# Attention stage of a hybrid decoder layer: which value products run whole in f32 (two key tiles in five, or every second one)

## What is computed

```python
s = einsum('bgrqd,bgnd->bgrqn', qi, ck) * scale
p_c = masked_softmax(s, cmp_end[None, :] <= t[:, None])
o_c = einsum('bgrqn,bgnd->bgrqd', p_c, cv)          # 63 compressed blocks
...
p_s = masked_softmax(s, smask[:, :, None])
o_s = einsum('bgrqk,bgqkd->bgrqd', p_s, vsel)       # all causal keys (16 blocks of 64 = SEQ)
...
p_w = masked_softmax(s, wmask)
o_w = einsum('bgrqk,bgkd->bgrqd', p_w, vwi)         # window of 512 keys
...
o = gates[..., 0:1] * o_c + gates[..., 1:2] * o_s + gates[..., 2:3] * o_w
```

## Time and profile before

| | before |
|---|---|
| median of 3 runs | 1686.25 us (1686.22 to 1688.09) |
| the profiled execution's own time | 1685.26 us |
| its span, first to last instruction | 1683.5 us |
| PE busy | 1620.0 us, 96% |
| DVE busy | 1021.6 us, 61% |
| ACT busy | 627.1 us, 37% |
| granted PE clock, mean over the span | 0.987 |

### The profile page before, as it was taken

The page is one execution under the profiler, slowest core; times in us unless marked ns, Lnnn a source line. Parts: engine busy times, 40 slices in busy tenths (PEclk is TensorE's granted clock), DMA queues, the critical chain, the costliest instruction groups (busy, mean ns, idle before and its releaser), DMA issues.

```text
span 1683.5 us, 22018 instructions
## 1 busy us (share of the span) xinstructions
PE 1620.0 (96%) x8157; PEld 1324.6 (79%) x8157; DVE 1021.6 (61%) x1871; ACT 627.1 (37%) x1173; POOL 77.9 (5%) x126
## 2 busy tenths in 40 slices
PE   8899999998789999999999999999999999999997
PEld 6688888888666777678888888888888888888885
DVE  6833556565599999863355565655556565556432
ACT  6214434344577777761231221221122122124221
POOL 0111212121000000000000000000000000000000
PEclk9899999999799999999999999999999999999999
DMA  5433323226000000060121211121121111122000
GB/s 199 131 101 113 100 95 111 81 71 228 26 23 14 17 10 4 1 238 1 38 75 38 67 45 37 38 74 37 37 75 37 37 44 68 37 76 100 25 38 38
DMA packets 48987, 110.60 MB, mean 66 GB/s; under 512 B 8848, under 2 KB 17040, under 8 KB 48912
## 3 DMA queue, kind: packets, MB, share of 16 engines
q1 hardware_dynamic: 41488, 85.47, 15.3%
q0 software_dynamic: 7424, 24.12, 4.3%
HBM read 89.65 MB, written 19.92 MB: 65 GB/s over the span
## 4 chain that ended last, share of the span: by engine, by line
PE 87%; DVE 5%; ACT 2%; issue 2%; DVEq 0%; POOLq 0%; POOL 0%; ACTq 0%
PE ps L1461 27%; PE ps L1115 14%; PE ps L1117 14%; PE ps L1116 14%; PE ps L1261 4%; PE ps L1377 3%; PE ps L1334 2%; PE ps L1340 2%; PE ps L1448 1%; PE ps L1379 1%; PE ps L1120 1%; PE ps L1284 1%; PE ps L1380 1%; PE ps L1342 1%; DVE nb L1867 1%
## 5 line engine op out<-in xcount | busy, mean ns | idle before, releaser
L2005 DVE TENSOR_TENSOR h<-h,ps 128x512 f32<-128x512 f32 x336 | 224.3, 686 | 137.9 <-PE ps L1117 136.2
L1461 PE MATMUL ps<-hth,wuh 128*128 128x512 f32 x672 | 206.9, 389 | 0.0
L1461 PE MATMUL ps<-hth,wul 128*128 128x512 f32 x672 | 206.9, 389 | 0.0
L1461 PE MATMUL ps<-htl,wuh 128*128 128x512 f32 x672 | 206.8, 389 | 0.0
L1115 PE MATMUL ps<-wh,xth 128*128 128x512 f32 (+1 forms) x448 | 185.8, 415 | 15.8 <-DVE wl L1595 14.3
L1117 PE MATMUL ps<-wh,xtl 128*128 128x512 f32 (+1 forms) x448 | 170.7, 381 | 0.0
L1116 PE MATMUL ps<-wl,xth 128*128 128x512 f32 (+1 forms) x448 | 169.8, 379 | 0.0
L1059 ACT ACTIVATE ffh<-ffa 128x1024 fp32r<-128x1024 f32 x22 | 23.3, 1061 | 358.4 <-DVE ffa L2032 358.4
L1461 PEld LDWEIGHTS ps<-hth,wuh 128*128 128x128 f32 x672 | 126.1, 188 | 26.2
L1461 PEld LDWEIGHTS ps<-hth,wul 128*128 128x128 f32 x672 | 126.1, 188 | 26.2
L1461 PEld LDWEIGHTS ps<-htl,wuh 128*128 128x128 f32 x672 | 126.1, 188 | 26.2
(11 more groups left out here) (270 smaller groups left out, 3147.8 us busy)
## 6 DMA issues: line engine op xcount, KB each, us to landing
wuraw<-in_w_up SPq DMA_DIRECT2D x44, 512.0 KB, 5.1
wraw<-in_w_in SPq DMA_DIRECT2D x48, 256.0 KB, 3.3
proj_d<-stage POOLq DMA_DIRECT2D x48, 256.0 KB, 2.3
wdraw<-in_w_down SPq DMA_DIRECT2D x22, 512.0 KB, 3.6
rin<-proj_d POOLq DMA_DIRECT2D x32, 256.0 KB, 4.4
xraw<-in_xt SPq DMA_DIRECT2D x16, 256.0 KB, 6.7
owraw<-in_w_out SPq DMA_DIRECT2D x8, 512.0 KB, 5.5
h<-in_x SPq DMA_DIRECT2D x1, 4096.0 KB, 15.5
```

The costliest lines, as they stand in the source:

```text
L1461: mm = nc.tensor.matmul(ps[:, 2 * part + half, :], w_, x_[:, k, half * 512:(half + 1) * 512], start=(k == 0 and i == 0), stop=(k == NK - 1 ...
L2005: nc.vector.tensor_tensor(hh, hh, ps[:, 4 + o_ % 4, :], ALU.add).then_inc(dn_add, 1)
```

## The change

```diff
         def whole(st):
...
-            return st[0] == "turn_p" and st[2] % 5 in (0, 2)
+            return st[0] == "turn_p" and st[2] % 2 == 0
```

## The result

| | before | after |
|---|---|---|
| median of 20 runs | 1686.49 us (1685.21 to 1689.19) | 1692.07 us (1689.18 to 1694.02) |
| ratio after/before | | 1.0028, 95% interval 1.0021 to 1.0035 |
| profiled execution's span | 1683.5 us | 1690.7 us |
| granted PE clock, mean over the span | 0.987 | 0.984 |

The change made the kernel slower by 0.28%, that is 4.7 us by the ratio (1686.49 x 0.0028). The forecast was +0.6 us with a range up to 1691.3 us; the time went where the first rival, "PE pays everywhere", had it (+5.0 us). On the 1686.25 us that the prediction started from, the ratio gives 1691.0 us: inside the range, but by 0.3 us, and only because its upper edge was the rival's price. The forecast case by itself ended at 1689.5 us, so that the number lies in the range is in part luck.

The account below looks back on a forecast made before the run. PE was taken to bound the kernel overall, with DVE holding views 2 to 7. Early -0.9 us and late +1.5 us gave +0.6 us, 1686.9 us for the median, with an 8 in 10 range of 1683.0 to 1691.3 us.

Parts of the forecast that it names:

- PE pays everywhere: First rival, views 2 to 7: nothing of DVE's relief arrives, 14 exchanges cost +5.0 us, 1691.3 us; chance 0.21.
- The forecast case: Whole kernel: the recorded sum, +0.6 us to 1686.9 us, own range 1684.0 to 1689.5 us; chance 0.62.
- The two regimes: Views 2 to 7: DVE idle 4.9 of 95.6 us; views 8 to 15: DVE idle 24.9 of 178.9 us.
- DVE holds views 2 to 7: Early views: DVE busy 90.75 of 95.6 us, its low part a link of the chain before PE's next query product.
- PE's price of an exchange: PE, 14 views from t = 1: whole product instead of split pair costs 0.36 us each, 5.0 us in all.
- The estimate of 0.43 us: PE, per exchange: two passes more than a split pair, 512 columns each at 2.4 GHz; 6.0 us for all 14.
- The sum: Views 2 to 15: PE's 0.36 us and DVE's 0.69 us per exchange weighted by chain shares, together +0.6 us.
- Early stretch: Views 2 to 7: six exchanges, PE and DVE/ACT loop each weighted 0.45, -0.9 us from 95.6 us.
- Late stretch: Views 8 to 15: eight exchanges, PE weighted 0.82, low part 0.15, +1.5 us on 178.9 us.
- DVE gives it all back: Second rival: low parts pace early views (-4.1 us), late views hide longer products; 1682.1 us, or 1676.6 us; chance 0.13.
- A new wait: Third rival, late views: alternation makes PE meet `ptl` too early, 8 x 0.9 = 7.2 us, 1694.1 us; chance 0.04.
- The rings: Places of `ptw` and `pth`, reused four tiles on: free before the next copy, priced at nothing.

Follow-up runs that it names:

- PE's side alone: Kernel before, but in 14 views tile 4's low part is made and unused, PE making one full f32 product of the high part; 1692.44 us, ratio 1.0032.
- DVE's side alone: Kernel before, but in 14 views tile 4's low part is made for 128 of 512 columns, PE's products unchanged; 1687.23 us, ratio 1.0001.

## Where the prediction held and where it failed, point by point

- **Where the kernel is bound.** The two regimes were read from DVE's idle time, 0.6 to 1.1 us a view early and more later. The reading "DVE holds views 2 to 7" held for views 2 and 3 only. The chain of views 4 to 6 by itself lies on PE lines for 62%; the row of views 2 to 7 together, 42%, hid that.
- **PE's price of an exchange.** Taken: 0.36 us, from 0.32 to 0.40. Measured: 0.395 us a view in views 8 to 15 (3.16 / 8), at the upper end; over 14 exchanges this is 0.5 us. The 0.32 us was a misreading: between two start times of a whole product one sees not all of its cost, because behind a transpose it also starts later. PE before, a pair and a whole product each between two transposes:

```profile
662.30 0.60 PE L1261 MATMUL ps<-cst,prob 128*128 128x128 f32 x4
662.66 0.47 PE L1379 MATMUL ps<-pth,av 128*128 128x512 f32 x1
662.97 0.39 PE L1380 MATMUL ps<-ptl,av 128*128 128x512 f32 x1
663.20 0.60 PE L1261 MATMUL ps<-cst,prob 128*128 128x128 f32 x4
...
667.81 0.61 PE L1261 MATMUL ps<-cst,prob 128*128 128x128 f32 x4
668.25 1.02 PE L1377 MATMUL ps<-ptw,av 128*128 128x512 f32 x2
669.11 0.60 PE L1261 MATMUL ps<-cst,prob 128*128 128x128 f32 x4
```

From transpose to transpose it is 663.20 - 662.30 = 0.90 us with a pair and 669.11 - 667.81 = 1.30 us with a whole product, 0.40 us more. The estimate of 0.43 us from the four passes of the Trainium skill ("FP8 and Floating Point Precision", section TensorE Precision Notes) is 0.03 us above the measured price, as far off as the 0.36 us on the other side.
- **The sum, the step that failed.** Each side was weighted by the share of the chain that its engines hold: PE 0.45 and 0.82, the low part 0.45 and 0.15. The runs show 1.0 for PE from view 4 on, and 0 for the low part. In views 2 and 3 both were near 0.4 (0.3 of 0.8 us for PE, 0.5 of 1.4 us for the low parts). A share tells how much of the chain lies on DVE, not whether the low part that goes is one of its pieces. The pieces of the chain of the earlier trace rows that are low parts, views 2 to 7:

```profile
472.77 0.58 DVE ptl L1813
...
475.61 0.69 DVE ptl L1813
...
478.54 0.68 DVE ptl L1813
...
484.10 0.69 DVE ptl L1813
...
491.27 0.68 DVE ptl L1813
...
514.14 0.69 DVE ptl L1813
...
557.33 0.69 DVE ptl L1813
...
561.34 0.68 DVE ptl L1813
```

By their order in DVE's timeline these are tiles 1, 3 and 4 of view 2, 1 and 4 of view 3, 1 of view 5, 6 and 8 of view 7. Tile 4, the one exchanged in the experiments, stands there in views 2 and 3 alone, and only in these views was its low part worth anything. The change takes tiles 6 and 8 of view 7 away too, but that view is only 0.07 us shorter than with PE's side alone (18.94 and 19.01 us): PE's path beside it is about as long. With weights of 1 and 0 from view 4 on and the measured -0.2 us for views 2 and 3, 12 x 0.395 - 0.2 = 4.5 us; the price and the -0.2 us come from the same profile, so this shows that the account closes and is no test of it.
- **Early stretch.** Forecast -0.9 us, measured +1.35 us without the clock (-0.19 + 1.54). Relief came in views 2 and 3 alone, 0.5 us of the 1.4 us removed there. The longer products cost 0.3 us there, and from view 4 on 0.39 us a view.
- **Late stretch.** Forecast +1.5 us, measured +3.2 us. The signs for it (DVE idle up, PE idle as before) came as written; DVE idle rose to 32.3 us.
- **Rivals.** "PE pays everywhere" is what happened, at 4.5 to 4.7 us; its sign, PE's waits for `prob` in views 2 to 7 staying near 4.2 us, came out between, at 3.3 us in 8 places: it fell in views 2 and 3 (from 2.8 to 1.8 us) and stayed at 1.4 us in views 4 to 7. "DVE gives it all back" fell with DVE's side alone; the reading after the Trainium skill ("Perfetto Trace Analysis", section Identifying the Most-Contended Engine) that DVE, as the engine with the higher occupancy, is the one to relieve did not hold from view 4 on, not even with DVE 95% busy and PE's weight loads at 44.62 of 68.00 us; tested on tile 4. "A new wait" did not come: 1.8 us in 2 places before and after.
- **Rings and clock.** The rings cost nothing, as written. That the clock was left out was a gap: low-clock stretches of 3.4 us, 1.5 us each, come and go in the same kernel. The sum was not touched by it, the comparison of single profiles was. All seven profiles whose long low stretch began between 428.8 and 429.4 us had two further ones in views 1 to 3; of the profiles where it began at 430.1 us or later, five in number with before, one had any. In the change and in most of the experiments the long stretch begins before the first instruction that differs (after 468 us). Whether the change makes the longer form more frequent is open: of its 27 runs 20 had a mean clock of 0.985 or less, of the 74 of before beside the experiments 37.

## What to carry to other kernels

Where two engines are both nearly full, relieving one gives nothing as long as the other path is as long, while work added to either costs: in full on the engine whose path is the longest, in part on the other. Do not weight a change by shares of the chain. Look whether the very instruction that goes is a piece of it, and ask each side for itself (take the work away on one engine, leave the other alone). Price an instruction from the start of the one before it to the start of the one behind it. An engine's idle time tells roughly how much it can still take, not what its relief is worth. Choose such a balance by stretch and not once for the kernel: in the views where PE was the pace and DVE had 2.8 us or more to spare (10, 12, 13, 14), one whole tile fewer gave 0.4 us each, and with a rule for each view the kernel was faster than with either rule for all.

## What the runs showed that was not expected

- A low-clock stretch of 3.4 us costs 1.5 us in views 2 and 3, and its place moves between executions of one kernel (473.5 or 487.4 us).
- With the softmax gone (view 15), the split form's latency, with two places for its tiles, decides: six exchanges that save PE 2.4 us of work made the view 2.8 us longer.
